# Differential attention: the weighted sum of the two exponent maps split between VectorE and GpSimd

## What is computed

```python
def diff_attend(q, k, v, lam):
    s = jnp.einsum('bqhmd,bkhmd->bhmqk', q, k).astype(jnp.float32) * (A_QK ** -0.5)
    p = jax.nn.softmax(s, axis=-1)
    a = p[:, :, 0] - lam * p[:, :, 1]
    return jnp.einsum('bhqk,bkhd->bqhd', a, v.astype(jnp.float32))
```

## Time and profile before

| | us |
|---|---|
| median of three runs | 1701.52 (1701.49 to 1704.73) |
| the profiled execution, its own time | 1706.78 |
| its span in the trace | 1705.0 |
| the attention stage, exponents first to last start | 374.9 to 504.7 |
| mean granted TensorE clock of the execution | 0.973 of full |

### The profile page before, as it was taken

One profiled execution on the slowest core, in us unless ns is written; L12 is line 12 of the kernel. 1 busy time (PEld: TensorE's weight loads), 2 busy tenths in 40 slices (PEclk: granted clock), 3 DMA queues, 4 the chain that ended last, 5 costly groups with the idle time before them and its releaser, 6 DMA issues. The chain is left out here.

```text
span 1705.0 us, 29716 instructions
## 1 busy us (share of the span) xinstructions
PE 1558.1 (91%) x12501; PEld 1320.5 (77%) x12501; DVE 748.8 (44%) x1256; ACT 684.9 (40%) x1106; POOL 419.5 (25%) x106
## 2 busy tenths in 40 slices
PE   3899999879886999998989999977879899999998
PEld 3788888777775878997878897845767888888786
DVE  3410113849987531115874534448563333333002
ACT  3311112128884331106764344462253455554212
POOL 1422222200004043222022243200034144444442
PEclk9899999989997999999999999979999999999999
DMA  8444312034612022207320432000021222222221
GB/s 336 155 161 186 149 50 85 5 74 96 141 38 99 1 74 99 75 31 222 88 77 23 136 127 86 7 1 3 4 101 50 75 98 98 98 96 76 102 96 74
DMA packets 31429, 153.13 MB, mean 90 GB/s; under 512 B 6728, under 2 KB 8264, under 8 KB 16848
## 3 DMA queue, kind: packets, MB, share of 16 engines
q1 hardware_dynamic: 30000, 150.62, 26.9%
q10 hardware_dynamic: 1312, 0.80, 0.2%
HBM read 129.39 MB, written 2.10 MB: 77 GB/s over the span
## 5 line engine op out<-in xcount | busy, mean ns | idle before, releaser
L215 PE MATMUL banks<-even_token_parts,even_weight_parts 128*128 128x512 f32 (+1 forms) x1296 | 235.8, 342 | 0.0
L215 PE MATMUL banks<-ffn_token_parts,ffu_weight_parts 128*128 128x512 f32 (+1 forms) x1056 | 231.1, 381 | 2.6 <-POOL ffu_weight_parts L196 2.3
L215 PEld LDWEIGHTS banks<-ffn_token_parts,ffu_weight_parts 128*128 128x128 f32 x1056 | 192.7, 189 | 40.7 <-POOL ffu_weight_parts L196 2.5
L215 PEld LDWEIGHTS banks<-even_token_parts,even_weight_parts 128*128 128x128 f32 x1296 | 198.3, 188 | 32.7 <-issue 2.9
L196 POOL TENSOR_TENSOR ffu_weight_parts<-weight_chunk,ffu_weight_parts 128x2048 fp32r<-128x2048 f32 x22 | 101.5, 4616 | 162.8 <-ACT ffu_weight_parts L190 162.8
L196 POOL TENSOR_TENSOR out_half<-weight_chunk,out_half 128x2048 fp32r<-128x2048 f32 x12 | 56.8, 4755 | 334.7 <-ACT out_half L190 308.9
L196 POOL TENSOR_TENSOR even_weight_parts<-weight_chunk,even_weight_parts 128x2048 fp32r<-128x2048 f32 x16 | 73.7, 4607 | 226.6 <-ACT even_weight_parts L190 226.6
L2884 PE MATMUL banks<-ffd_weight_parts,ffn_f_parts 128*128 128x512 f32 x528 | 120.1, 389 | 1.6 <-PEq L2787 1.6
L2884 PEld LDWEIGHTS banks<-ffd_weight_parts,ffn_f_parts 128*128 128x128 f32 x528 | 99.0, 188 | 22.5 <-issue 2.0
L215 PE MATMUL banks<-sec_token_parts,sec_weight_parts 128*128 128x512 f32 (+1 forms) x528 | 115.7, 377 | 0.3 <-PEq L268 0.3
L2862 DVE SCALAR_TENSOR_TENSOR ffn_conv<-banks,b_ffn_taps,ffn_conv 128x511 f32<-128x511 f32 (+1 forms) x88 | 61.9, 745 | 114.5 <-ACT ffn_conv L2836 111.4
(11 more groups left out here) (444 smaller groups left out, 2795.8 us busy)
## 6 DMA issues: line engine op xcount, KB each, us to landing
weight_chunk<-in_ffn_up SPq DMA_DIRECT2D x22, 1024.0 KB, 4.8
weight_chunk<-in_w_in_even SPq DMA_DIRECT2D x16, 1024.0 KB, 6.8
even_pT<-in_w_mod SPq DMA_DIRECT2D x16, 1024.0 KB, 4.9
weight_chunk<-in_w_in SPq DMA_DIRECT2D x13, 1024.0 KB, 4.9
weight_chunk<-in_w_out SPq DMA_DIRECT2D x12, 1024.0 KB, 4.9
weight_chunk<-in_w_in_odd SPq DMA_DIRECT2D x12, 1024.0 KB, 5.0
weight_chunk<-in_ffn_down SPq DMA_DIRECT2D x11, 1024.0 KB, 4.8
front_w<-in_w_mod SPq DMA_DIRECT2D x8, 1024.0 KB, 12.4
```

What stands on the lines that cost most here:

```text
L215: m = self.nc.tensor.matmul(o, w, env.tok[:, tp, k, a:b], start=n == 0, stop=n == 3 * KD - 1)
```

## The change

The one VectorE instruction of `combine` becomes two on two engines. `scale(u)` on VectorE multiplies the exponents of the second map by the ratio, in place, with a tensor_scalar that reads one tensor. GpSimd then adds both maps into the buffer that `turn` reads, and raises `combined` in VectorE's place. The wait for `turned` moves to GpSimd with it. A new semaphore, `weighted`, leads from VectorE to GpSimd. `weight` computes the same ratio by a tensor_scalar with two pointer operands, which reads one tensor, instead of a scalar_tensor_tensor, which reads two.

```diff
-                dve.sem_inc(combined, 2)
...
-                    st.inc(nc.vector.scalar_tensor_tensor(
+                    st.inc(nc.vector.tensor_scalar(
                         ratio[:], recip[:, u % 8, 1:2], env.neg_lam[:], sums[:, u % 2, 0:1], ALU.mult, ALU.mult))
 
-                def combine(u):
+                def scale(u):
                     _, _, n, _ = unit(u)
                     dve.wait_ge(dve_step, st.base + st.n)
-
-                    dve.wait_ge(turned, u + 1)
-                    nc.vector.scalar_tensor_tensor(
-                        at[u % 2][:, 0:n], ex[u % 2][1][:, 0:n], ratio[:], ex[u % 2][0][:, 0:n], ALU.mult, ALU.add
-                    ).then_inc(combined, 1)
+                    nc.vector.tensor_scalar(ex[u % 2][1][:, 0:n], ex[u % 2][1][:, 0:n], ratio[:], None, ALU.mult).then_inc(weighted, 1)
...
                     if 1 <= u <= UNITS:
-                        combine(u - 1)
+                        scale(u - 1)
+
+            @block.gpsimd
+            def _(pool):
+                pool.sem_inc(combined, 2)
+                for u in range(UNITS):
+                    _, _, n, _ = unit(u)
+                    pool.wait_ge(weighted, u + 1)
+                    pool.wait_ge(turned, u + 1)
+                    nc.gpsimd.tensor_tensor(at[u % 2][:, 0:n], ex[u % 2][1][:, 0:n], ex[u % 2][0][:, 0:n], ALU.add).then_inc(combined, 1)
```

More of the change, by code:

```diff
@@ L888, in stage_diff_attention @@
         max_ready, exp_done, combined, turned = [sem(f"max{m}") for m in range(2)], [sem(f"exp{m}") for m in range(2)], sem("combined"), sem("turned")
-        turned_out, pv_ready, o_out, dve_step = sem("turned_out"), sem("pv"), sem("o_out"), sem("step")
+        turned_out, pv_ready, o_out, dve_step, weighted = sem("turned_out"), sem("pv"), sem("o_out"), sem("step"), sem("weighted")
         T0, O0 = 4 * BANK, 6 * BANK
```

## The result

The changed kernel takes 1749.5 us (median of four runs, 1747.78 to 1751.52) against 1701.51 for the kernel before (median of four, 1698.67 to 1704.73): a ratio of 1.0268, with an interval of 1.0249 to 1.0287. That is 46 us slower by the ratio (0.0268 of 1702) and 48 by the medians. I had forecast 27 more, and a range that ended at 1741: the direction was right, the size too small by some 20 us.

The account below looks back on a forecast made before the run. The attention stage was taken to run on a loop through three nearly full engines: 2.23 us a group added, 0.46 absorbed, 1.77 paid in 15 groups (26.6), plus 0.8 at the end, so 1701.5 + 27, about 1728 us; range 1714 to 1741.

Parts of the forecast that it names:

- VectorE's gain: VectorE freed of 0.75 us a group, at most 12 us, most staying on other full engines; faster rival 1689, chance 0.03.
- 0.46 to 0.48 us of slack: Before a full unit's transposes: combine ends about half a microsecond early, so 0.46 a group of added latency is absorbed.
- the forecast point of no loss at 0.74: For 768 columns, an addition up to 0.74 us keeps scale, hop and addition within combine and its slack.
- The addition: GpSimd's sum of both maps: 1.83 us for 768 columns (lower bound 1.47), 0.73 for 256.
- The hop: Each hand-over between engines, such as VectorE to GpSimd: 0.10 us.
- the higher rival: VectorE's 128x2 reciprocal also held by GpSimd's addition: 10.61 us a group, 37 us paid, 1739; chance 0.12.
- The scale of unit B: Second full unit's scale on VectorE, held by the shared port until add(A) ends, stretched to 1.5 us or more.
- The loop with the port held: Main case: scale(A) through both additions, TensorE and maxima to scale(A'), 9.94 us a group, 1.77 paid; chance 0.63.
- add(B) 1.83 and hop 0.10; turn(B) 0.61 (424.42 to 425.03): Loop step: the second full unit's transposes follow its addition and hand-over, and take 0.61 us.
- all falling together to three quarters: Sign in the profile after: busy shares of TensorE, VectorE and ScalarE in the attention stage drop together to three quarters.
- pv(A) 1.34 and scores(B') 0.66: Loop steps on TensorE after turn(B): product with v 1.34 us, then scores to their first maximum 0.66.
- the rival without it: Scale(B) not held, so a loop over ScalarE decides: 9.33 us a group, 1719; port weaker or addition shorter, chance 0.19.

Follow-up runs that it names:

- e6: The changed kernel with GpSimd adding only the first 256 of 768 columns of a full unit: 1703.5 us, ratio 1.0001 to the kernel before.
- e4: The kernel before with only the ratio changed to the one-stream tensor_scalar: 1703.6 us, ratio 1.0005.
- e5: The changed kernel with four and two dead identity products on TensorE ahead of the transposes of each group's two full units: 1725.7 us, ratio 1.0120.
- e8: The kernel before, combine still on VectorE, with one more round between exponents and transposes and more buffers: 1730.2 us, ratio 1.0140.
- e3: The changed kernel with scale and addition as two instructions both on VectorE, GpSimd idle: 1718.4 us, ratio 1.0093 to the kernel before.
- e10: The changed kernel with small TensorE filler (four and two dead products a group) and the second full unit's scale cut to 2 columns: 1723.2 us, ratio 1.0108.

## Why the prediction was right in direction and wrong in size

**Right.** That VectorE's gain is worth nothing, as far as e6 can show it. That combine had 0.46 to 0.48 us of slack: an addition of 0.73, just below the forecast point of no loss at 0.74, cost nothing (e6). The addition, 1.83 and 0.73 forecast, took 1.81 and 0.72. The hop took 0.08, forecast 0.10. The reciprocals were not held, which takes the higher rival away; that the time came out above that rival's 1739 has another cause. Scale took 0.61 in place of 0.65 and 0.34 in place of 0.45. The ratio took 0.27, nearly double the 0.15 of its row (0.22 before), and was free as assumed (e4).

**Right in kind, wrong in size.** The scale of unit B was held, but it was forecast "stretched to 1.5 or more" and took 0.93 to 0.99; its end came 0.4 us after the addition's, not 0.65. The loop with the port held was 9.94 on paper, and is 9.60 with the clock at full (e5): 1.43 a group over before instead of 1.77, 23 us in 16 groups, and e5 measured 20 to 21 over its own before. A smaller point: the estimate that the prediction draws from the 4497 ns of the Trainium skill (GPSIMD Engine Reference, section 3.1) comes to 1.69 us for 768 of 2048 columns, not to some 1.8; the addition took 1.81.

**Wrong.** The step that failed is "add(B) 1.83 and hop 0.10; turn(B) 0.61 (424.42 to 425.03)": that turn(B) starts when add(B) has ended, and that TensorE's durations can be carried over from rows at full clock, as if the waits that the same sum put before them had no effect on them. The prediction even forecast the busy shares "all falling together to three quarters" and did not ask what the waits do to the clock. (VectorE and ScalarE fell to two thirds; TensorE stayed at 82% only by taking longer over the same work.) In the trace after, turn(B) took 1.00, and it was not add(B) that released it, but TensorE itself, which was late: the steps from turn(A) to turn(B), which the sum left out as hidden, take 1.12 + 0.86 + 1.28 = 3.26, where e5 without its filler has 0.60 + 0.45 + 0.71 = 1.76. The way over add(B) was 2.31 from the start of turn(A) (447.23 to 449.49, and 0.05 for the hop). So 0.95 more went by until turn(B) began, and turn(B) lasted 0.40 longer than in e5: 1.35, which is the 1.33 between 9.60 and 10.93. The other two steps that the sum has there, pv(A) 1.34 and scores(B') 0.66, came out as forecast, since the clock was full again by then.

The same by the whole way round TensorE. At full clock, without filler, it would be 9.04: in the steps of e5 from start to start, add(A) to turn(A) 1.87, turn(A) 0.60, pv 0.45, scores 0.71, turn(B) 0.60, pv(A) 1.34, scores(B') 0.66, the maximum and the ratio 1.26, the second maximum 0.86, the scale 0.69. The low clock adds 1.90 to four of them, and 9.04 + 1.90 = 10.94, where the walk above had 10.93.

How the forecast missed by 21 us is then this, for the 15 groups that it counted. The clock adds 1.33 a group, 20 us. The loop at full clock was taken 0.34 too long, which takes 5 off. That makes 15, and the spans of the traces grew by 41 against the 27 forecast, 14 more. The other 7 lie between the profiled executions and the medians, and no run explains them. A side effect is that the hold of scale(B), by which my sum was 0.61 a group longer than that of the rival without it, is not paid in the changed kernel: turn(B) comes 1 us after add(B) has ended. That is read from the trace of the changed kernel, and no run tests it.

The trace of before could have warned of the clock. Three stretches at the start of the stage there, in the columns of the windows above:

```profile
370.00:376.00 6.00, 0.01 (x1) 0.01 (x1) 4.43 (x6) 3.64 (x6) 0.00 (x0) 0.56 0.95 197
376.00:384.00 8.00, 6.20 (x20) 4.74 (x21) 6.18 (x13) 4.88 (x12) 0.00 (x0) 0.50 0.12 25
386.00:396.00 10.00, 8.46 (x60) 6.90 (x59) 9.02 (x19) 8.29 (x20) 0.00 (x0) 1.00 0.47 98
```

TensorE did nothing from 370 to 376, its clock fell, and it was still at 0.50 until 384, though by then TensorE was busy for most of the time; from 386 on it is 1.00. So the row shows that idle time in this stage costs the clock. It does not show that pauses of about a microsecond are enough, which only the trace after did. A sum with the steps from turn(A) to turn(B) at half clock would have been 10.93 a group, 2.76 over before, which is 41 us in 15 groups and 1743; which steps would be the slow ones could not be read beforehand, and with all of TensorE's steps slow the sum is higher still.

## What to carry to other kernels

Before giving a step of a software pipeline to a slower engine, measure how early its result is now (the time between its end and the start of what uses it); the new latency, hand-over included, is free up to that and paid in every round beyond it, and a relieved engine may give nothing back if it was not alone on the loop. Then ask what the new waits do to TensorE: where they put idle time into each group, recompute its steps with the clock at half, those of its own way round as well as those on the loop, and take that as the upper case. A filler of dead products of just the size of the wait can tell the two costs apart in one run; size it by a trace, since one that outlasts the wait costs more than the clock gives.

## What the runs showed of the hardware

TensorE lost its full clock with idle stretches of only 0.5 and 1.0 us in the group of 10.9 shown above, and in e8 it fell after ones of 0.73 and 0.52, though not each time (1.00 from 422 to 424.5 us, 0.55 from 424.5 to 434.8); in e3, with at most 0.58 and 0.31 in a group of 9.0, it kept it. 96 products of the identity in otherwise idle time took the stage from 0.81 to 1.00 and gave back 24 us. A two-column tensor_scalar on VectorE is held by a GpSimd addition as one of 768 columns is (0.60 us, to the addition's end), while a two-column reciprocal is not (0.15 to 0.17 us). The held one of 768 columns ended 0.41 us after the addition (447.59 against 447.18), sooner than the 0.61 that it takes alone. The Trainium skill (SBUF — State Buffer, Who interferes with whom) names tensor_scalar among the operations that can take both ports; the trace of e10 agrees, with its two columns held for 0.60 us.
